# Turning queries and keys by small DMAs instead of products, one slot later, in a two-block transformer kernel

## The reference, cut to what matters

```python
def partial_rope(x, cos, sin):
    half = ROT_DIM // 2            # 8
    x1 = x[..., :half]
    x2 = x[..., half:ROT_DIM]
    r1 = x1 * cos - x2 * sin
    r2 = x2 * cos + x1 * sin
    return jnp.concatenate([r1, r2, x[..., ROT_DIM:]], axis=-1)
```

## Time and profile before

| | us |
|---|---|
| median of 3 runs (1545.2 to 1547.62) | 1545.45 |
| the profiled execution | 1545.34 |
| its span | 1543.2 |
| PE busy | 1395.3 (90%) |
| DVE busy | 1063.1 (69%) |
| ACT busy | 771.4 (50%) |
| POOL busy | 294.0 (19%) |

### The profile page before, as it was taken

One profiled execution on the slowest core, in us unless ns is written; L12 is line 12 of the kernel. 1 busy time (PEld: TensorE's weight loads), 2 busy tenths in 40 slices (PEclk: granted clock), 3 DMA queues, 4 the chain that ended last, 5 costly groups with the idle time before them and its releaser, 6 DMA issues.

```text
span 1543.2 us, 22378 instructions
## 1 busy us (share of the span) xinstructions
PE 1395.3 (90%) x8042; PEld 1023.8 (66%) x8042; DVE 1063.1 (69%) x2252; ACT 771.4 (50%) x1648; POOL 294.0 (19%) x297
## 2 busy tenths in 40 slices
PE   7999998999998778778778799999999998999998
PEld 5988996444443223223222288888999987999997
DVE  2988656766667667666665578447777786577776
ACT  3555533544444444444444364746555567455555
POOL 0111002454544444444444200000000010000000
PEclk9999999999999999999999999999999999999999
DMA  9775646999999999999999944234555531345553
GB/s 397 293 271 219 244 150 265 426 412 424 426 427 427 427 427 427 427 427 427 427 427 427 427 152 164 83 110 164 188 172 185 190 127 66 117 171 191 187 179 126
DMA packets 62586, 432.93 MB, mean 281 GB/s; under 512 B 7072, under 2 KB 7584, under 8 KB 12192
## 3 DMA queue, kind: packets, MB, share of 16 engines
q0 software_dynamic: 41616, 285.76, 44.4%
q1 hardware_dynamic: 20160, 145.37, 26.5%
q10 hardware_dynamic: 720, 0.62, 0.1%
HBM read 430.67 MB, written 1.05 MB: 280 GB/s over the span
## 4 chain that ended last, share of the span: by engine, by line
PE 56%; DMA 20%; DVE 10%; ACT 10%; issue 3%; POOL 0%; another core or an unknown queue 0%; ACTq 0%; DVEq 0%; POOLq 0%
PE banks L700 25%; PE banks L1119 14%; DMA arena<-in_peer_uv,experts 9%; DMA tok_b<-in_peer_uv,experts 5%; DMA tok_a<-in_peer_uv,experts 4%; PE banks L1294 3%; PE banks L1261 3%; DVE wlow L1838 3%; PE banks L737 3%; ACT diag L1601 2%; PE banks L961 2%; ACT scores L1460 1%; ACT whigh L1338 1%; ACT L1593 1%; ACT L1575 1%
## 5 line engine op out<-in xcount | busy, mean ns | idle before, releaser
L1119 PE MATMUL banks<-arena,diag 128*128 128x512 f32 x780 | 381.5, 622 | 81.1 <-ACT diag L1601 81.1
L2266 DVE CUSTOM_DVE_ANT_0 arena<-arena,scores 128x1024 f32<-128x1024 f32 x200 | 245.0, 1225 | 159.1 <-DMA arena<-in_peer_uv,experts 155.9
L1119 PEld LDWEIGHTS banks<-arena,diag 128*128 128x128 f32 x780 | 139.9, 193 | 311.2 <-ACT diag L1601 188.6
L1838 DVE TENSOR_TENSOR wlow<-wring,whigh 128x1024 fp32r<-128x1024 f32 x232 | 273.4, 1220 | 85.9 <-ACT whigh L1338 85.7
L1786 POOL DMA_INDIRECT arena<-in_peer_uv,experts x200 | 212.4, 1062 | 367.1 <-PE banks L1119 259.9
L1338 ACT ACTIVATE whigh<-wring 128x1024 fp32r<-128x1024 f32 x232 | 232.2, 1048 | 89.7 <-DMA wring<-in_w_down 34.2
L700 PE MATMUL banks<-f_high,whigh 128*128 128x256 f32 x720 | 205.2, 285 | 7.1 <-DVE wlow L1838 4.5
L1593 ACT ACTIVATE dots<-dots 128x1 f32<-128x1 f32 x256 | 51.8, 202 | 308.2 <-DVE dots L2266 308.0
L700 PE MATMUL banks<-f_low,whigh 128*128 128x256 f32 x720 | 203.7, 283 | 0.0
L700 PE MATMUL banks<-f_high,wlow 128*128 128x256 f32 x720 | 203.7, 283 | 0.0
L700 PE MATMUL banks<-a_high,whigh 128*128 128x256 f32 x512 | 151.6, 296 | 3.6 <-DVE a_low L1846 2.1
(11 more groups left out here) (285 smaller groups left out, 2386.9 us busy)
## 6 DMA issues: line engine op xcount, KB each, us to landing
wring<-in_w_up SPq DMA_DIRECT2D x44, 1024.0 KB, 4.8
wring<-in_w_down SPq DMA_DIRECT2D x22, 1024.0 KB, 4.8
wring<-in_w_in SPq DMA_DIRECT2D x17, 1024.0 KB, 7.0
wring<-in_w_qkv_a SPq DMA_DIRECT2D x12, 1024.0 KB, 5.0
arena<-in_w_mod SPq DMA_DIRECT2D x8, 1024.0 KB, 16.3
arena<-in_w_mod_t POOLq DMA_DIRECT2D x16, 512.0 KB, 5.7
hT<-in_w_mod_t POOLq DMA_DIRECT2D x16, 512.0 KB, 5.5
wring<-in_peer_w_q SPq DMA_DIRECT2D x5, 1024.0 KB, 4.9
```

What stands on the lines that cost most here:

```text
L1119: mm = nc.tensor.matmul(banks[:, 2 + 2 * b + half, :], diag[:, n % DIAGS, :], ring[ROW_PLACE[n]][:, D + half * 512:D + (half + 1) * 512], ...
L1838: V.tensor_tensor(low, w, high.bitcast(F32), ALU.subtract).then_inc(w_split, 1)
L2266: V.tensor_tensor_reduce(out=ring[ROW_PLACE[n]][:, 0:D], in0=ring[ROW_PLACE[n]][:, 0:D], in1=h2tok[:, b, :], scale=1.0, scalar=0.0, op0=AL ...
```

## The change

Eleven of the thirteen rotation products are left out (all but r = 8 and r = 12). POOL issues four small DMAs for each of these chunks, which copy 8 rows of 2 KB from `raw` to their exchanged place in `tmp`; the other rows of `tmp` are zeros, which POOL writes once for each layer. The sign moves from the constant matrix into the frequency, and by it into the sine table. DVE's sine product then reads `tmp` and not PSUM. In the order of the slots, DVE's rotation of chunk n-2 stands at slot 2n; before, that of chunk n-1 stood at slot 2n+1. Rotations 8 and 12 stay where they were. Two waits of PE on `roped2` go, which kept the PSUM banks of the rotation products apart from those of the probabilities.

```diff
         if d < 8:
-            c[base + d + 8, C_ROT2 + m] = -1.0
+            c[base + d + 8, C_ROT2 + m] = 1.0
...
-            c[m, C_FREQ] = np.float32(500000.0) ** (np.float32(-2 * (d % 8)) / np.float32(16))
+            c[m, C_FREQ] = (-1.0 if d < 8 else 1.0) * np.float32(500000.0) ** (np.float32(-2 * (d % 8)) / np.float32(16))
...
-        def rot_bank(r):
-
-            return {7: 6, 11: 6, 12: 0}.get(r, 4 + r % 2)
+        turned_by_pe = {8: 4, 12: 0}
...
             def turn_probs(g):
-                if g is plans[1]["groups"][0] or g is plans[2]["groups"][0]:
-
-                    pe.wait_ge(roped2, 7 if g is plans[1]["groups"][0] else 11)
...
                     pe.wait_ge(proj2_read, (None, 9 + g["first"] // 4, 17)[plan["which"]])
-                    pe.wait_ge(roped2, (None, 8, 12)[plan["which"]])
...
                     mm_at = pending.pop()
-                    pe.wait_ge(proj2_read, mm_at + 1)
-                    if r >= 2:
+                    if r in turned_by_pe:
+                        pe.wait_ge(proj2_read, mm_at + 1)
                         pe.wait_ge(roped2, r - 1)
-                    if rot_bank(r) == 0:
-                        pe.wait_ge(proj2_read, m - 1)
-                    nc.tensor.matmul(banks[:, rot_bank(r), :], const[:, C_ROT2:C_ROT2 + P], raw[:, r % 2, :],
-                                     start=True, stop=True).then_inc(rot2_made, 1)
+                        if turned_by_pe[r] == 0:
+                            pe.wait_ge(proj2_read, m - 1)
+                        nc.tensor.matmul(banks[:, turned_by_pe[r], :], const[:, C_ROT2:C_ROT2 + P], raw[:, r % 2, :],
+                                         start=True, stop=True).then_inc(rot2_made, 1)
                     r += 1
...
+            def clear_turned(l, ready, count):
+
+                pool.wait_ge(ready, count)
+                nc.gpsimd.memset(tmp[:, :, :], 0.0).then_inc(rot_clear, 1)
+                pool.wait_ge(rot_clear, l + 1)
+
+            def turn_by_dma(r, m):
+
+                pool.wait_ge(proj2_read, m + 1)
+                if r >= 2:
+                    pool.wait_ge(roped2, r - 1)
+                for head in (0, HD):
+                    for to, of in ((head, head + 8), (head + 8, head)):
+                        pool.dma_start(tmp[to:to + 8, r % 2, :], raw[of:of + 8, r % 2, :]).then_inc(rot2_in[r % 2], 16)
+
+            clear_turned(0, ps_made, PEER_HEADS)
+            for r in range(8):
+                turn_by_dma(r, r)
+            clear_turned(1, ff_ready, FF_STEPS)
             sums = hT[:, 0:2, :].rearrange("p k t -> p (k t)")
...
+            for r in range(9, 12):
+                turn_by_dma(r, len(proj2[0]) + r - 8)
             pool.wait_ge(wo_made, 4 * LAYERS)
...
                     step.mark(V.tensor_tensor(dst, src, cosb2, ALU.mult))
-                    dve.wait_ge(rot2_made, r + 1)
-                    step.link(V.tensor_tensor(t, banks[:, rot_bank(r), :].rearrange("p (k t) -> p k t", k=2), sinb2,
-                                              ALU.mult))
+                    if r in turned_by_pe:
+                        dve.wait_ge(rot2_made, 1 + (r > 8))
+                        dve.wait_ge(rot_clear, l + 1)
+                        at = banks[:, turned_by_pe[r], :].rearrange("p (k t) -> p k t", k=2)
+                    else:
+                        turned_in_by[r % 2] += 64
+                        dve.wait_ge(rot2_in[r % 2], turned_in_by[r % 2])
+                        at = t
+                    step.link(V.tensor_tensor(t, at, sinb2, ALU.mult))
                     V.tensor_tensor(dst, dst, t, ALU.add).then_inc(roped2, 1)
...
                     n, j = divmod(slot, 2)
-                    if j == 1 and 1 <= n < chunks2:
-                        rope_chunk(n - 1)
-                    if slot == 2 * chunks2:
+                    if j == 0 and l + 2 <= n < chunks2:
+                        rope_chunk(n - 2)
+                    if l == 1 and slot == 3:
+                        rope_chunk(0)
+                    if l == 1 and slot == 2 * chunks2:
                         rope_chunk(chunks2 - 1)
                     attention_slot(plan, slot)
```

More of the change, by code:

```diff
@@ L391, in build @@
         rot2_made, roped2 = sem("rot2_made"), sem("roped2")
+        rot_clear, rot2_in = sem("rot_clear"), [sem("rot2_in_a"), sem("rot2_in_b")]
         dup2_made, dup2_read = sem("dup2_made"), sem("dup2_read")
@@ L2347, in _ @@
             m = r = 0
+            turned_in_by = [0, 0]
             for l in range(LAYERS):
```

## The result

The changed kernel took 1559.17 us (median of 4 runs, 1557.38 to 1559.52) against 1545.34 us for the kernel before (4 runs): ratio 1.0082, 95% interval [1.0066, 1.0098], by which it is 12.7 us slower (10.2 to 15.1). The forecast was 1554.0 us with a range from 1548.5 to 1559.5: the median lies inside it, 0.3 us from its upper end. The profiled execution took 1557.38 us, 12.0 us more than that of before.

A forecast was written before the change was run, and what follows sets the result against it. PE bounds the kernel with DVE's and ACT's in-order loop close behind; moved rotations make that loop the bound. Lateness of 4.7 us (layer 0) plus 3.8 (layer 1), swallowing 9.5 us of removed products: 1545.45 + 8.5 = 1554.0 us, range 1548.5 to 1559.5.

The forecast's parts named there:

- the sum: Both layers: 4.7 us lateness in layer 0 plus 3.8 in layer 1, 8.5 us slower; chance 0.52 without late DMAs or clock falls.
- late DMAs: Rival: at 11.6 us per chunk, chunks 4 and 5 come 1.7 us late each, 3.4 us more, 1557.4 us; chance 0.10.
- Chunk loop: Layer 0: the rounding, split, rotation, copy loop closes at 5.9 us against PE's 5.75; 3.0 us stall ahead of chunk 6.
- Score loop: Layer 0, slots 14, 16, 18: rotations ahead of the even maxima make them late by 1.9, 3.1 and 5.0 us.
- score 0: Layer 0's first score waits for rotation 4 until 956.3 us, a gap of 2.4 us on PE.
- Score 1's gap: Layer 0: a new PE gap of 3.3 us ahead of the second score.
- The DMAs are hidden: POOL's four DMAs turn a chunk in 5.6 us, within a cover of 9.9 us, so they cost nothing.
- Triples of the same length: DVE's rotation triples keep their length with both inputs in SBUF; another length, 13 x 0.1 us, would be 1.3 us.
- lock-out: DVE's two-port modes could block POOL's DMA issue, 12.4 us for four; tensor_tensor has no such mode, so probably not.
- the rival of the falling clock: PE's clock falls in layer 0's new gaps, 1.6 us a fall; one or two give 1555.6 to 1557.2 us; chance 0.20.
- done well before: The rotations named by the removed `roped2` waits in `turn_probs` and `weigh` finish early, so removing these waits gains nothing.
- PE stays the bound: Rival: the full gain of eleven removed products, 9.5 us, is kept, 1536.0 us; chance 0.08.

The follow-up runs named there:

- gaps_filled: Changed kernel with useless constant products put into four of PE's new gaps, three in layer 0 and one in layer 1: 1555.96 us, ratio 1.0061 to before.
- dmas_doubled: Changed kernel with eight DMAs for each turned chunk in place of four, the sine product waiting for all eight: 1558.00 us, ratio 1.0080 to before.
- before_late_split: Kernel before, with odd slots' splits held until after the next slot's maximum, from slot 13 in layer 0 and 7 in layer 1: 1540.80 us, ratio 0.9969.
- dma_old_late_split: Changed kernel with rotations back in their old slots and odd slots' splits held until after the next slot's maximum: 1534.26 us, ratio 0.9927 to before.
- after_late_split: Changed kernel with the splits of odd slots held until after the next slot's maximum: 1541.45 us, ratio 0.9975 to before.

## Why the prediction was right, and by how much it was off

**How near the edge.** By the ratio the loss is 12.7 us against the 8.5 of the sum. The range was wide enough only because its upper end took in late DMAs and two falls of the clock; the DMAs were not late, and the clock fell oftener instead. That the time stayed inside by 0.3 us is partly luck; the path and the sign are not.

**The mechanism stood, step by step.** To compare with before, 1.93 us are added to the times of after in layer 0.
- *Chunk loop.* Predicted period 5.9 us, measured 5.96. Predicted stall ahead of chunk 6: 3.0 us, measured 3.12. Chunk 4's copy was foreseen to end at 945.0 us; chunk 6 started at 945.33.
- *Score loop.* Even maxima of slots 14, 16, 18 begin 2.8, 3.9 and 5.8 us later than before (before: 960.34, 970.34 and 980.35 us). Predicted were 1.9, 3.1 and 5.0. From one to the next they grow by 1.1 and 1.8 us (predicted 1.2 and 1.9); a nearly constant 0.8 to 0.9 us lies under them.
- *That 0.9 us is the clock.* The sum took ACT's rounding of chunk 9 at 956.9 us; it was at 957.8 and waited for its load, which waits for the end of chunk 6 on PE. The chain of waits gives chunk 6 as below, 7.41 us in place of 5.76, in the stretch where the clock was 0.55. In gaps_filled, where this fall is gone, the same three maxima, counted from the first chunk, begin 2.1, 3.3 and 5.1 us later than before, within 0.2 us of the prediction. It also explains score 0: predicted wait 2.4 us, measured 1.04, since PE came later.

```profile
943.40 7.41 PE banks L699 x48
...
950.83 5.05 DMA wring<-in_w_qkv_a
```

- *Score 1's gap.* Predicted 3.3 us, measured 3.69.
- *The DMAs are hidden.* Predicted 5.6 us for a chunk, with a landing of 3.5 us as lower bound; four issues took 2.1 us and landing 2.3 us, 4.4 us in all. The predicted cover of 9.9 us for chunk 4 was 9.8 (copy ended 943.35, sine product at 953.16). The clears took 0.96 us each, and the first lies in a stretch that was shorter than before.
- *Triples of the same length.* 684 ns with both inputs in SBUF, 685 to 692 with one in PSUM.

The Trainium skill's page DMA: Bandwidth & Descriptors (section Anatomy of one DMA — SWDGE (gpsimd) path) gives about 2.0 us fixed for a DMA on this path; an estimate for 16 KB by its fit is hardly more. The trace agrees in the median, 2.3 us, but some landings took up to 5.0. The lock-out of the Trainium skill that the prediction weighed (SBUF — State Buffer, section SBUF: two separate sides) did not occur: POOL issued at 518 ns while DVE's tensor_tensor ran beside (four issues in 2.05 us from 943.63 us on, across the split at 944.32), near the 527 ns of the earlier trace rows, which agrees with that page's section Who interferes with whom, by which tensor_tensor has no two-port mode and with two SBUF inputs contends only with what GpSimd reads.

**The term that was mis-sized: the granted clock.** The sum put nothing for it and the rival one or two falls of 1.6 us. There were six stretches at a low clock, 31 us in all where before had 3, and during them PE was busy for 28 us, which at full clock would have been about half that. Not all of these 14 us reach the end: filling four gaps took 17 us of low time away and gave back some 3 us of run time. So the likeliest case as I named it, my sum without falls, is not what happened; the rival of the falling clock is, with more falls than I had priced. What is left after filling, +6.0 us in layer 0 and +5.1 in layer 1 against predicted 4.7 and 3.8, may be partly the three falls that stayed. I could not split it further: two kernels of the same time, dmas_doubled and the changed one, differ by some 2 us in a stretch.

**A cost that I had at nothing.** The removed `roped2` waits were worth nothing in the old slots and are 13.9 us of idle PE in the new ones (11.9 in layer 0, 2.0 in layer 1). The prediction's result is unhurt, since the change removes them, but its reason ("done well before") was true only of the old order.

**What the removed products were worth.** The prediction had 9.5 us of products swallowed by lateness, which makes the move 18 us dear. Measured, the products give 2.6 us in the old slots and the move costs 15.3 us with DMAs, clock included. The rival "PE stays the bound" fails even in the old slots: there the second score's gap grew from 0.94 to 2.71 us.

## What to carry to other kernels

When an engine works strictly in program order, ask of each instruction what its neighbours wait for, and not only when its own result is due: the same 1.9 us of VectorE cost less where the next score ran on TensorE meanwhile, and cost 1.1 to 2.1 us each between a split and a maximum (by the three maxima of gaps_filled). Ask too which buffer its result sets free: one split later in the chunk loop, the same instruction held up the copies and cost 6.0 us up to the first score. Work taken off the busiest engine pays only as far as the next loop behind it allows; here 9.5 us became 2.6, and moving one other instruction (the split) out of the way of the maxima raised the gain to 11. Before pricing a removed wait at nothing, check it in the new order too.

## What the runs showed of the hardware

- A transfer of 8 rows by 2 KB within SBUF, issued by POOL, landed in 1.7 to 5.0 us (median 2.3) with the weights' loads running beside it; issuing took 518 ns in the median. Of 88 of them in place of 44, neither half was slower (518 ns, median 1.9 us).
- In gaps_filled 17 us less of low time went with some 3 us less of run time (2.3 to 3.2 by the ratios, with overlapping intervals), well under half of the low time. Why so little is not shown.
- The clock fell at short gaps. In the changed kernel it was 1.00 over 938 to 943 us and fell to 1.2 GHz at 943.1, late in the 3.12 us of idleness that end at 943.40. In the kernel before it fell at 1308.7 us, as PE took up work at the end of a gap of 2.69 us. In before_late_split and dma_old_late_split, whose longest gap in these stretches is 1.62 us, no fall was seen. The longest gap alone does not decide, though: towards the end of layer 1 both have gaps of 1.37, 1.12 and 0.91 us, and with the same three gaps (1.38, 1.12 and 0.91 us) the clock of after_late_split fell at 1305.3 us.
